# Two transformer blocks in one kernel: where the weight rings begin, modulo 128 bytes

## What is computed

```python
def reference(x, ...):
    x = first_block(x, c, ada_w, ...)      # RWKV-7 mixer, then a convolutional FFN
    return second_block(x, w_in_2, ...)    # attention + HGRN2, then a squared-ReLU MLP

# first block, its dense products
r, k, v = jnp.einsum("nbtd,nde->nbte", x_rkv, w_rkv)     # 3 x [256,2048] @ [2048,2048]
y = _rwkv7_scan(r, decay, k, v, -kk, kk * ah)            # 32 heads, 256 steps
y = (y * g) @ w_o                                        # [2048,2048]
u = _causal_dwconv(h @ ffn_w_in, conv_w, conv_b)         # [2048,11008]
f = (silu(gate) * val) @ ffn_w_out                       # [5504,2048]

# second block, its dense products
proj = h @ w_in                                          # [2048,5376]
mixed = concatenate([attn, rnn]) @ w_out                 # [2048,2048]
u = relu(h @ w_up)                                       # [2048,8192]
y = (u * u) @ w_down                                     # [8192,2048]
```

## Time and profile before

| what | us |
|---|---|
| median of 3 runs (lowest to highest) | 2891.71 (2889.53 to 2897.59) |
| the profiled execution | 2891.93 |
| its span, first to last instruction | 2890.0 |
| dense stage of layout a | 130 to 431 |
| scan (layout s) | 431 to 851 |
| dense stage of layout b, with attention and HGRN2 beside it | 852 to 2007 |
| dense stage of layout d | 2047 to 2872 |

### The profile page before, as it was taken

The page is one execution under the profiler, slowest core; times in us unless marked ns, Lnnn a source line. Parts: engine busy times, 40 slices in busy tenths (PEclk is TensorE's granted clock), DMA queues, the critical chain, the costliest instruction groups (busy, mean ns, idle before and its releaser), DMA issues.

```text
span 2890.0 us, 44956 instructions
## 1 busy us (share of the span) xinstructions
PE 2732.2 (95%) x19186; PEld 2306.1 (80%) x19186; DVE 1870.2 (65%) x2436; ACT 1310.6 (45%) x1768; POOL 177.6 (6%) x167
## 2 busy tenths in 40 slices
PE   6999987889889899999999989999989999999997
PEld 1488876767768788888888878888978888888886
DVE  3787656777754766767867666567657556566565
ACT  1244443353334655345445555556554444343443
POOL 0120002011001000000000021000020000000001
PEclk9999998998989999999999999999999999999999
DMA  9766752232336364865775544543445555655562
GB/s 374 275 231 233 236 182 80 81 113 85 107 120 194 114 193 157 310 189 189 253 234 184 182 153 155 172 146 102 132 146 185 194 190 176 203 190 189 175 204 88
DMA packets 289207, 514.05 MB, mean 178 GB/s; under 512 B 10096, under 2 KB 122736, under 8 KB 288880
## 3 DMA queue, kind: packets, MB, share of 16 engines
q1 hardware_dynamic: 286016, 500.21, 51.9%
q0 software_dynamic: 2560, 7.90, 0.8%
q10 hardware_dynamic: 432, 3.07, 0.3%
HBM read 508.91 MB, written 2.10 MB: 177 GB/s over the span
## 4 chain that ended last, share of the span: by engine, by line
PE 83%; DVE 7%; ACT 5%; issue 3%; DMA 2%; POOL 0%; DVEq 0%; SPq 0%; ACTq 0%
PE ps L804 46%; PE ps L811 23%; DMA RAWa<-in_ada_w 2%; PE ps L950 1%; ACT WHb L1241 1%; PE ps L773 1%; PE ps L713 1%; PE ps L945 1%; PE ps L935 1%; DVE WLb L1772 1%; PE ps L902 1%; PE ps L743 1%; PE ps L1001 1%; DVE ACCs L1755 1%; DVE WS L2028 1%
## 5 line engine op out<-in xcount | busy, mean ns | idle before, releaser
L804 PE MATMUL ps<-XB,WHb 128*128 128x512 f32 x2304 | 650.1, 402 | 24.1 <-issue 11.0
L1772 DVE TENSOR_TENSOR WLb<-RAWb,WHb 128x2048 fp32r<-128x2048 f32 (+1 forms) x196 | 426.7, 2192 | 258.7 <-ACT WHb L1241 258.5
L1772 DVE TENSOR_TENSOR WLd<-RAWd,WHd 128x2048 fp32r<-128x2048 f32 x144 | 328.3, 2290 | 258.8 <-ACT WHd L1241 258.8
L1241 ACT ACTIVATE WHb<-RAWb 128x2048 fp32r<-128x2048 f32 (+1 forms) x196 | 356.8, 1833 | 299.5 <-PE ps L811 264.5
L804 PEld LDWEIGHTS ps<-XB,WHb 128*128 128x128 f32 x2304 | 398.7, 191 | 87.2 <-issue 18.5
L1241 ACT ACTIVATE WHd<-RAWd 128x2048 fp32r<-128x2048 f32 x144 | 274.0, 1914 | 338.8 <-PE ps L811 338.8
L811 PEld LDWEIGHTS ps<-XB,WLb 128*128 128x128 f32 x2304 | 357.4, 190 | 50.7
L811 PE MATMUL ps<-XB,WLb 128*128 128x256 f32 x2304 | 370.1, 282 | 0.0
L804 PE MATMUL ps<-XD,WHd 128*128 128x512 f32 x1280 | 353.5, 398 | 8.2 <-issue 6.1
L804 PE MATMUL ps<-FB,WHd 128*128 128x512 f32 x1024 | 280.9, 396 | 0.0
L804 PEld LDWEIGHTS ps<-XD,WHd 128*128 128x128 f32 x1280 | 218.2, 188 | 38.4 <-issue 6.4
(11 more groups left out here) (334 smaller groups left out, 3529.6 us busy)
## 6 DMA issues: line engine op xcount, KB each, us to landing
RAWb<-in_ffn_w_in SPq DMA_DIRECT2D x168, 512.0 KB, 5.0
RAWd<-in_w_up SPq DMA_DIRECT2D x64, 1024.0 KB, 5.3
RAWd<-in_w_down SPq DMA_DIRECT2D x64, 1024.0 KB, 5.2
RAWa<-in_ada_w SPq DMA_DIRECT2D x48, 1024.0 KB, 7.3
RAWa<-in_rwkv_w_rkv SPq DMA_DIRECT2D x48, 1024.0 KB, 6.0
RAWb<-in_ffn_w_out SPq DMA_DIRECT2D x36, 1024.0 KB, 5.3
RAWs<-in_ada_w SPq DMA_DIRECT2D x32, 1024.0 KB, 5.0
RAWb<-in_w_in SPq DMA_DIRECT2D x44, 512.0 KB, 5.0
```

Source lines behind the costliest of these rows:

```text
L804: pe.matmul(banks[tile_bank[i]][:, :], WH[tag][:, w, o:o + P], acts(k), start=(k == 0), stop=False)
L1241: act.activation(WH[tag][:, n % WN, 0:size], RAW[tag][:, slot_of[i], 0:size], ACT.Copy).then_inc(s_wh, 1)
L1772: dve.tensor_tensor(WL[tag][:, n % WN, 0:size], RAW[tag][:, slot, 0:size], WH[tag][:, n % WN, 0:size].bitcast(F32), ALU.subtract).then_inc ...
```

## The change

The rings WH and WL of layouts a and b get 32 bytes of unused space ahead of them (`step_a`, `step_b`), and the filler of layout d grows from 10,304 to 10,400 bytes, which is 81 x 128 + 32. The distances become 32 modulo 128 in all three (from 0, 0 and 64). RAWa and RAWb stay where they are, RAWd lies behind WLd and moves with it. The moving tiles stay where they are. No instruction, semaphore, wait or transfer is added, removed or moved, and the order on each engine is what it was.

```diff
@@ -329,6 +329,7 @@
         raw_ring(st_raw, "a")
         st_r = ExitStack()
         XA = sb(st_r, "XA", [P, ND, 2 * T], FR)
+        sb(st_r, "step_a", [P, 8])
         weight_rings(st_r, "a")
         st_r.close()
         st_raw.close()
@@ -362,6 +363,7 @@
         st_b = ExitStack()
         raw_ring(st_b, "b")
         XB = sb(st_b, "XB", [P, ND, 2 * T], FR)
+        sb(st_b, "step_b", [P, 8])
         weight_rings(st_b, "b")
         st_b.close()
         st_e = ExitStack()
@@ -377,7 +379,7 @@
         XD = sb(st_g, "XD", [P, ND, 2 * T], FR)
         FB = sb(st_g, "FB", [P, 16, 2 * T], FR)
         UM = sb(st_g, "UM", [P, 4, T])
-        sb(st_g, "clear_of_e", [P, 2576])
+        sb(st_g, "clear_of_e", [P, 2600])
         weight_rings(st_g, "d")
         raw_ring(st_g, "d")
         st_g.close()
```

## The result

The changed kernel takes 2908.4 us, the median of 6 runs (2903.53 to 2911.17), against 2891.54 us before. The ratio is 1.0053, with a 95% interval of 1.004 to 1.0066. The prediction was 2876 us, with a range of 2845 to 2902: the kernel became slower by 17 us where 16 us less were forecast.

What follows compares the result with a forecast made beforehand. The prediction took TensorE's dense matmul spacing to bound the kernel. Terms of -15.7 us (layouts a and b), 0 (layout d) and 0 (conversions) took 2891.93 us to 2876 us, ratio 0.9946, range 2845 to 2902.

Steps and rivals of the forecast that it cites:

- What bounds the kernel: Whole kernel: TensorE's dense matmuls, busy 95% of the span; time is mostly their count times their spacing.
- That the other engines have slack, so that a change of spacing arrives in full,: Dense stages: ScalarE, VectorE and DMA are not late, so a group's gain or loss reaches the end almost in full.
- The cause is the distance and not the place: Dense groups: spacing goes with ring-to-moving-operand distance, not the tile; 64 instead of 0 gives 16.7 ns a group.
- the rival that placement does nothing: Layouts a, b, d: two independent read ports, so 32 bytes do nothing; 2892 us, chance 0.06.
- One p for all three layouts: Dense groups of a, b, d: one spacing p under distance 32 modulo 128, taken as 1.386 us, break-even at 1.397.
- breaking point: Dense groups: any spacing at 32 not framed by those of 0 (1.403 us) and 64 (1.386 us) breaks the prediction.
- Relation 32 costs what 64 does: Layouts a, b, d: distance 32 modulo 128 gives 1.386 us per group, as 64 does; 2876 us, chance 0.38.
- The term of -15.7 us in a and b: Layouts a and b, 940 groups going from 1.4032 to 1.3865 us: -15.7 us, bounds -50 and +16.
- The term of layout d: Layout d, 576 groups going from distance 64 to 32: 0, bounds -21 and +9.6, or +19 us at 1.420.
- worse than both: All three layouts: 32 costs more than 0 and 64, 1.420 us per group; +35 us, 2927 us, chance 0.12.
- as 0: 32 costs what 0 costs: a and b gain nothing, d loses 9.6 us; 2901.5 us, chance 0.13.
- The range: Whole kernel: 2845 to 2902 us, leaving out "worse than both" and the lower half of the better-than-64 case, about 0.2.

Runs made afterwards that it cites:

- all64: Kernel before with 64 bytes unused ahead of the rings of layouts a and b, so distance 64 in all three: ratio 0.9958, 2879.3 us.
- swap: Kernel before with pads giving distance 160 in a and b, 32 in d: 1.413 us per group in a and b, 1.403 in d; 2907.7 us.
- split: Kernel before with pads putting XB at distance 64, FA 160, XD 192, FB 96, layout a 224: 1.387, 1.413, 1.384, 1.410, 1.400 us per group.
- The scan: Four kernels, the kernel before with pads of other sizes, for distances 96 to 416: spacings 1.383 to 1.413 us, repeating every 256 bytes.

## Why the prediction was wrong

*What bounds the kernel* was right. The count of groups times the spacing gives the change within a microsecond: 940 x 0.9 + 576 x 26.5 ns = 0.8 + 15.3 = 16.1 us, where the medians differ by 16.9. The three stages of the profiled executions differ by 18.5, of which 1.5 us are the two slow-clock groups in layout a; the rest, 0.9, is not traced.

*That the other engines have slack, so that a change of spacing arrives in full,* was right: ScalarE waits for L813 350.2 us in d, 11 us more than in the earlier trace rows, with the conversions unchanged.

*The cause is the distance and not the place* was right. It rested on the kernel before alone, where d differs from a and b in more than the distance; all64, swap and split have shown it. The Trainium skill ("TensorE: Matmul & The Clock Gate", "Step-by-step: what each phase is for") says that the next weight load takes no read bandwidth from the running matmul, and the prediction drew from it the rival that placement does nothing. That rival is refuted: split has 1.413 against 1.387 us from one ring. Whether the load is what costs the time is argued and not shown.

*One p for all three layouts* was the first step that failed. The prediction took the text of the change, "32 modulo 128", for the variable, though the sizes that the section on the kernel adds up give 32,800 and 80,032 bytes. The sum had one unknown where there were two, 1.403 for 940 groups and 1.413 for 576. It had named as its breaking point a p that the two known relations don't frame; d's 1.413 lies outside them.

*Relation 32 costs what 64 does* was the second. The term of -15.7 us in a and b was +0.8. The reason given was that only a common beginning costs, since the highs hardly differ between 0 and 64. That premise was read from medians. Four highs do take 928 ns at both, but from start to start the single ones are 234, 234, 232 and 228 ns for XB at 0, and 226, 236, 231 and 236 for FB at 64: they differ by up to 8 ns, and the sum hides it. The scan refutes the conclusion: 32, 96, 160 and 224 are off the common beginning and have 1.400 to 1.413, and with 160 the highs are dearer too (four in 932 ns). Two sums that agree had been read as a law. The rows supported no value between 1.35 and 1.42 over another. The size of the term was also 7% too large: over all groups 0 and 64 differ by 15.6 ns, and not the 16.7 of two stretches read to 0.01 us.

*The term of layout d*, 0 with bounds of -21 and +19 us, measured +15.3: inside the bounds, near the end that the rival "worse than both" had. That rival, with chance 0.12, is what happened in d, and "as 0" is what happened in a and b. Its chance was set low for L912, whose 379 ns say nothing here: L858 and L912 lie at 0 and 32 modulo 256 too, two distances that the float32r stream doesn't tell apart either.

*The range* ended at 2902 because "worse than both" was left outside. The bounds from the rows allowed 2927, and no row of this stream spoke against it.

## What to carry to other kernels

Where TensorE streams float32r operands and the load of the next weights runs beside every matmul, measure the spacing from start to start for each pair of tiles and look at the distance of the two operands modulo 256 bytes. Here two distances 32 bytes apart (160 and 192) differ by 2.1% in spacing, and the best distances are narrow, so they must be measured and not interpolated. An edit stated modulo some number is an assumption about the period: write down the full distances of every operand pair, and compare layouts that already differ before trusting it.

## What the runs showed of the hardware

- At full clock the spacing of 4 x 512 + 4 x 256 columns of float32r runs from 1.383 to 1.413 us by the distance modulo 256, 2.2%; tiles at one distance differ by at most 3 ns. The shape of the dependence is not explained. That it comes from the weight load beside the moving stream is argued: VectorE and ScalarE are ruled out above, and RAW, where the DMAs write, stayed in place in a and b while their spacing changed. It is not shown, since no run left the loads out.
- At the granted clock of 0.50, the 1.2 GHz level, it isn't seen. In the 14 kernels 50 groups follow a pause of TensorE, of 4.45 us or more, and run wholly at 0.50. They cover all eight distances of the table, and from the first high to the end of the lows they took 2.695 to 2.700 us, with 425 to 428 ns between highs (the first left out) and 212 to 218 between lows. At full clock distances 64 and 160 are 26 ns apart. One of these groups, in layout d after a pause of 6.05 us, at distance 64 (before), then at 160 (after):

```profile
2150.42:2153.12 2.70, 2.70 (x9) 2.31 (x10) 2.70 (x4) 1.24 (x5) 1.33 (x2) 0.50 0.00 0
```

```profile
2156.30:2158.99 2.69, 2.69 (x8) 2.31 (x9) 2.69 (x4) 1.24 (x5) 1.32 (x2) 0.50 0.00 0
```

- Plain fp32 matmuls at distances 0 and 32 had the same 379 ns. As the float32r stream has 1.402 and 1.403 us at these two, whether plain fp32 depends on the distance stays open.
